# First attention and gate units of a two-block network: softmax, turned copies and a polynomial rearranged

## The reference

```python
# sliding-window attention, 32 query heads of 64, 4 key/value heads, blocks of 128 tokens
logits = jnp.where(valid, q @ k * (HEAD_DIM ** -0.5) + bias, NEG_INF)
m = jnp.maximum(jnp.max(logits, axis=-1, keepdims=True), sink)
e = jnp.exp(logits - m)
p = e / (jnp.sum(e, axis=-1, keepdims=True) + jnp.exp(sink - m))
o = p @ v
# the recurrent unit's gate
y_a = (rec * jax.nn.gelu(lru_gate, approximate=True)) @ w_lru_out
```

## Time and profile before

| | us |
|---|---|
| median of 3 runs | 2642.24 |
| lowest, highest | 2641.92, 2642.67 |
| the profiled execution | 2639.21 |
| its span in the profile | 2637.3 |
| granted TensorE clock, mean | 0.999 |

### The profile page before, as it was taken

The page is one execution under the profiler, slowest core; times in us unless marked ns, Lnnn a source line. Parts: engine busy times, 40 slices in busy tenths (PEclk is TensorE's granted clock), DMA queues, the critical chain, the costliest instruction groups (busy, mean ns, idle before and its releaser), DMA issues.

```text
span 2637.3 us, 35369 instructions
## 1 busy us (share of the span) xinstructions
PE 2612.8 (99%) x13718; PEld 2230.5 (85%) x13718; DVE 1840.2 (70%) x2519; ACT 1373.8 (52%) x2012; POOL 78.1 (3%) x136
## 2 busy tenths in 40 slices
PE   9999989999999999999999999999999999999998
PEld 7888878888888888888888888888888888888886
DVE  7876788888888786655665566676566566865665
ACT  5137766655444654454445445644655565445543
POOL 0000000000000000000000000100010001000000
PEclk9999999999999999999999999999999999999999
DMA  9995577788989696655565565565546646655463
GB/s 390 409 359 177 157 250 253 264 306 296 324 320 341 209 318 208 199 189 187 192 196 189 190 203 170 181 214 188 167 146 196 226 159 195 220 189 163 144 223 128
DMA packets 164727, 595.85 MB, mean 226 GB/s; under 512 B 19392, under 2 KB 20448, under 8 KB 164048
## 3 DMA queue, kind: packets, MB, share of 16 engines
q1 hardware_dynamic: 158544, 574.00, 64.1%
q0 software_dynamic: 6016, 19.59, 2.5%
HBM read 584.80 MB, written 3.47 MB: 223 GB/s over the span
## 4 chain that ended last, share of the span: by engine, by line
PE 90%; DVE 5%; ACT 3%; issue 1%; DMA 1%; SPq 0%; DVEq 0%; ACTq 0%
PE bank L839 27%; PE bank L881 26%; PE bank L893 14%; PE bank L844 13%; PE bank L856 2%; DVE both_w L1708 1%; PE pX L856 1%; PE pS L856 1%; PE pX L988 1%; PE pS L927 1%; ACT both_w L1255 1%; DMA raw<-in_w_vw 1%; PE pX L976 0%; PE pS L949 0%; DVE bank L2234 0%
## 5 line engine op out<-in xcount | busy, mean ns | idle before, releaser
L1708 DVE TENSOR_TENSOR both_w<-raw,both_w 128x1024 fp32r<-128x1024 f32 x848 | 1024.0, 1217 | 517.6 <-ACT both_w L1255 513.2
L1255 ACT ACTIVATE both_w<-raw 128x1024 fp32r<-128x1024 f32 x848 | 882.0, 1050 | 654.0 <-PE bank L844 407.1
L881 PE MATMUL bank<-H,both_w 128*128 128x512 f32 x3264 | 784.3, 391 | 0.1
L881 PEld LDWEIGHTS bank<-H,both_w 128*128 128x128 f32 x3264 | 599.3, 188 | 117.2 <-issue 1.3
L893 PE MATMUL bank<-H,both_w 128*128 128x256 f32 x3264 | 442.9, 285 | 0.7 <-DVE both_w L1708 0.7
L893 PEld LDWEIGHTS bank<-H,both_w 128*128 128x128 f32 x3264 | 424.4, 191 | 21.1 <-issue 2.0
L839 PE MATMUL bank<-both_w,H 128*128 128x512 f32 x1280 | 320.7, 393 | 0.4 <-DVE H L1711 0.3
L839 PEld LDWEIGHTS bank<-both_w,H 128*128 128x128 f32 x1280 | 238.6, 188 | 53.1 <-ACT both_w L1255 3.3
L839 PE MATMUL bank<-both_w,F 128*128 128x512 f32 x1024 | 253.1, 389 | 0.0
L1760 DVE SCALAR_TENSOR_TENSOR raw<-raw,CR 128x1024 f32<-128x1024 f32 x192 | 232.0, 1218 | 12.3 <-DMA raw<-in_ada 11.8
L839 PEld LDWEIGHTS bank<-both_w,F 128*128 128x128 f32 x1024 | 192.2, 188 | 39.9
(11 more groups left out here) (336 smaller groups left out, 2251.1 us busy)
## 6 DMA issues: line engine op xcount, KB each, us to landing
raw<-in_w_in SPq DMA_DIRECT2D x280, 512.0 KB, 3.7
raw<-in_w_ff SPq DMA_DIRECT2D x256, 512.0 KB, 4.1
raw<-in_ada SPq DMA_DIRECT2D x192, 512.0 KB, 5.6
raw<-in_w_out SPq DMA_DIRECT2D x96, 512.0 KB, 4.9
raw<-in_w_vw SPq DMA_DIRECT2D x64, 512.0 KB, 4.1
raw<-in_w_sig SPq DMA_DIRECT2D x64, 512.0 KB, 4.7
raw<-in_w_x SPq DMA_DIRECT2D x32, 512.0 KB, 10.3
raw<-in_w_lru_out SPq DMA_DIRECT2D x32, 512.0 KB, 4.7
```

Source lines behind the costliest of these rows:

```text
L881: ins = pe.matmul(out[i].rearrange("p (a s) -> p a s", a=2), whi[:, s, at_:at_ + 128], both[:, :, kt, :], start=(c == 0 and k == 0), stop= ...
L1255: act.activation(whi[:, s, 0:el.n], raw[el.slot][:, 0:el.n], ACT.Copy).then_inc(s_hi, 1)
L1708: dve.tensor_tensor(wlo[:, s, 0:n], raw[el.slot][:, 0:n], v32(whi[:, s, 0:n]), ALU.subtract).then_inc(s_lo, 1)
```

## The change

In the program's VectorE part, `softmax` with a sink reduces to the negated maximum at once (as the call without a sink did), takes the minimum with the negated sinks, and subtracts: three small instructions behind the bias step where there were four. The sinks are negated once, in place, in the first norm's stage. The two `inverse` calls of a block become one `inverse_both`, on both halves' columns, in the later of the two ticks. In the gate unit, 0.5 G1 (x^2 + G0/G1) x is formed as one instruction (x^2 + G0/G1) x, and the factor 0.5 G1 becomes the scale of the tanh.

In ScalarE's part, the two copies into PT move ahead of the exponentials of half 1, from tick 5 to tick 4. The scaling of half 0 moves from tick 5 to tick 0 of the next block, where both halves are now scaled together.

```diff
@@ ScalarE, attention
                 if 0 <= advance - 1 < NB:
-                    weigh(2 * advance - 1, 2 * advance - 1, S)
+                    for t in range(2):
+                        weigh(2 * advance - 2 + t, 2 * advance - 2 + t, 128 * (t + 1))
                 yield
...
                 yield from ticks(2)
-                for t in range(2):
-                    if advance < NB:
-                        exps(2 * advance + t, 2 * advance + t, 128 * (t + 1), True)
-                    yield
+                if advance < NB:
+                    exps(2 * advance, 2 * advance, 128, True)
+                yield
                 if 0 <= advance - 1 < NB:
...
                     act.activation(PT[:, 1, 0:2, :], pO[:, 256:512].rearrange("p (a q) -> p a q", q=128),
                                    ACT.Copy).then_inc(s_pt, 2)
                 if advance < NB:
-                    weigh(2 * advance, 2 * advance, 128)
+                    exps(2 * advance + 1, 2 * advance + 1, S, True)
+                yield
                 yield
@@ ScalarE, gate
-            act.activation(g1, g0, ACT.Tanh).then_inc(s_gt2, 1)
+            act.activation(g1, g0, ACT.Tanh, scale=0.5 * G1).then_inc(s_gt2, 1)
@@ VectorE, decay
+            sinks = vec[:, V_SINK:V_SINK + 32]
+            vc.add(dve.tensor_scalar(sinks, sinks, -1.0, None, ALU.mult))
@@ VectorE, softmax
-            t = vc.add(dve.tensor_reduce(mx, L, AX.X, ALU.max))
+            t = vc.add(dve.tensor_reduce(nm, L, AX.X, ALU.max, negate=True))
             dve.wait_ge(s_vc, t)
-            t = vc.add(dve.tensor_tensor(mx, mx, sink, ALU.max))
+            t = vc.add(dve.tensor_tensor(nm, nm, sink, ALU.min))
             dve.wait_ge(s_vc, t)
-            t = vc.add(dve.tensor_scalar(nm, mx, -1.0, None, ALU.mult))
+            dve.tensor_tensor(es, nm, sink, ALU.subtract).then_inc(s_mx, 1)
+
+        def inverse(a):
+            dve.wait_ge(s_ex, a + 1)
+            dve.reciprocal(SM[:, a % 4, 4, :], SM[:, a % 4, 2, :]).then_inc(s_rd, 1)
+
+        def inverse_both(b):
+
+            n = 2 * b % 4
+            rs, es, rd = (SM[:, n:n + 2, i, :] for i in (2, 3, 4))
+            dve.wait_ge(s_ex, 2 * b + 2)
+            t = vc.add(dve.tensor_tensor(rs, rs, es, ALU.add))
             dve.wait_ge(s_vc, t)
-            dve.tensor_tensor(es, sink, nm, ALU.add).then_inc(s_mx, 1)
-
-        def inverse(a, sink):
...
+            dve.reciprocal(rd, rs).then_inc(s_rd, 2)
@@ VectorE, attention
-                for t in range(2):
-                    inverse(2 * b + t, True)
-                    yield
+                yield
+                inverse_both(b)
+                yield
@@ VectorE, gate unit's evacuation
-                t = vc.add(dve.tensor_scalar(g0, g0, 0.5 * G1, 0.5 * G0, ALU.mult, ALU.add))
-                dve.wait_ge(s_vc, t)
-                dve.tensor_tensor(g0, g0, ps[:, :], ALU.mult).then_inc(s_gb, 1)
+                dve.scalar_tensor_tensor(out=g0, in0=g0, scalar=G0 / G1, in1=ps[:, :], op0=ALU.add, op1=ALU.mult).then_inc(s_gb, 1)
```

More of the change, by code:

```diff
@@ L1880, in softmax @@
             L, n = LP[:, jn % 3, :, 0:nk], a % 4
-            mx, nm, es = SM[:, n, 0, :], SM[:, n, 1, :], SM[:, n, 3, :]
+            nm, es = SM[:, n, 1, :], SM[:, n, 3, :]
             dve.wait_ge(s_qk, a + 1)
@@ L1897, in softmax @@
                 return
-            t = vc.add(dve.tensor_reduce(mx, L, AX.X, ALU.max))
+            t = vc.add(dve.tensor_reduce(nm, L, AX.X, ALU.max, negate=True))
             dve.wait_ge(s_vc, t)
-            t = vc.add(dve.tensor_tensor(mx, mx, sink, ALU.max))
+            t = vc.add(dve.tensor_tensor(nm, nm, sink, ALU.min))
             dve.wait_ge(s_vc, t)
-            t = vc.add(dve.tensor_scalar(nm, mx, -1.0, None, ALU.mult))
-            dve.wait_ge(s_vc, t)
-            dve.tensor_tensor(es, sink, nm, ALU.add).then_inc(s_mx, 1)
-        def inverse(a, sink):
-            rs, es, rd = SM[:, a % 4, 2, :], SM[:, a % 4, 3, :], SM[:, a % 4, 4, :]
-            dve.wait_ge(s_ex, a + 1)
-            if sink:
-                t = vc.add(dve.tensor_tensor(rs, rs, es, ALU.add))
-                dve.wait_ge(s_vc, t)
-            dve.reciprocal(rd, rs).then_inc(s_rd, 1)
+            dve.tensor_tensor(es, nm, sink, ALU.subtract).then_inc(s_mx, 1)
[7 more added lines that the diff above has]
+            t = vc.add(dve.tensor_tensor(rs, rs, es, ALU.add))
+            dve.wait_ge(s_vc, t)
+            dve.reciprocal(rd, rs).then_inc(s_rd, 2)
         def attention():
@@ L1971, in layer_jobs @@
                     elif job.a >= 0 and step == 1:
-                        inverse(job.a, False)
+                        inverse(job.a)
                 yield
```

## The result

| | median us | range | runs |
|---|---|---|---|
| before | 2642.45 | 2641.92 to 2644.05 | 4 |
| after | 2628.15 | 2627.65 to 2628.33 | 4 |

The ratio is 0.9945 with a 95% interval of 0.9927 to 0.9962: faster by 14.3 us. Forecast were 12.1 us, and 2630.1 us. The fast edge of the forecast's range, 2628.0, stood for a gain of 14.2 us, so the measured gain is just beyond it. The profiled execution of after took 2628.28 us, its span is 2626.4 us and its granted clock 0.999.

What follows compares the result with a forecast made beforehand. TensorE bounds the kernel, with 10.8 of its 24.5 idle us in the first attention. Waits 10.19, clock 1.67 and VectorE 0.25 sum to 12.11 us, so 2642.24 - 12.11 = 2630.1 us; range 2628.0 to 2635.5.

Steps and rivals of the forecast that it cites:

- All five waits: First attention, 310 to 550 us: TensorE's waits for L1358 ahead of L976 all go, 10.19 us.
- bounds of 1 to 2 us: VectorE's steps alone, without the moved copies, would bring about 1 to 2 us.
- no new wait: TensorE's transposes (L963): scaling both halves together adds no wait; bounds nothing or 0.5 us.
- the first place: Block 0, ahead of L976: copies into PT come in time, the 3.19 us wait goes, 0.6 us to spare.
- In the second: Transposes after the 3.94 us wait: the second scaling ends 0.5 to 1.3 us before TensorE comes.
- priced at 0.25 us: VectorE's shorter steps: the split that TensorE waited for at 328.25 us comes earlier, 0.25 us.
- the clock term: First attention, 391 to 396 us, behind the 3.94 us wait: the lowered clock goes with the wait, 1.67 us.
- clock luck: Rival: timed runs before met no fall (2631.8 us) or one at both long waits (2628.4); inside the forecast's 0.73.
- the offset of 3.03 us: Whole run: the median before lies 3.03 us above the profiled execution; the same difference was assumed after.
- not 13.7: VectorE's busy time over the run: 13.7 us less, 13.9 removed less 0.17 for negating the sinks.
- these prices: VectorE: the fused gate instruction takes L2246's time, no price; the merged reciprocal on 4 columns takes 0.17 us.
- nothing given back, and not slower: Rivals: DMA paces later weight stages, 2642 us (0.08 with no effect); joint reciprocal slips 5 us, 2656 us (0.05).

Runs made afterwards that it cites:

- e1_copies: Kernel before with only the two copies into PT moved ahead of the exponentials of half 1: 2630.05 us, ratio 0.9954.
- e11_order: Kernel before with all of ScalarE's new order, joint scalings included, VectorE's part old: 2630.15 us, ratio 0.9958.
- e9_filled: Kernel before with 7 and 8 products of unused result put into TensorE's two long waits: 2638.92 us, ratio 0.9989.
- e8_again: Kernel before, unchanged, for a second profiled execution: 2642.64 us.
- e10_again: Kernel before, unchanged, for a third profiled execution: 2640.31 us.
- e7_after: Kernel after, unchanged, run once more beside the kernel before: 2628.31 us, ratio 0.9948.
- e6_scaling: Kernel after with its scalings parted again, half 0 scaled at its old place in tick 5: 2631.31 us, ratio 0.9959.
- e2_vector: Kernel after with ScalarE's attention in the old order, so VectorE's steps alone: 2640.85 us, ratio 0.9997.
- e3_first: Kernel before with the copies into PT moved ahead in block 0 alone: 2637.26 us, ratio 0.9982.
- e4_second: Kernel before with the copies into PT moved ahead in block 2 alone: 2638.0 us, ratio 0.9983.
- e5_filled: Kernel before with 13 and 16 products of unused result put ahead of TensorE's two long waits: 2644.24 us, ratio 1.0008.

## Why the prediction was right and where it was wrong

**Right: the mechanism and its place.** All five waits of the earlier trace rows are gone, L1357 stands ahead of the second exponentials, and the stage is shorter by 12.1 us between the two profiled executions, as summed. e1_copies alone brings 12.0 us, and VectorE's steps alone 1.2 by the medians, in the bounds of 1 to 2 us that were set for them, though not told from nothing by the interval.

**Right, but by a smaller margin than it looks: no new wait.** In the first place 0.6 us to spare were worked out and 0.9 found. In the second, 0.5 to 1.3 us were worked out for the scalings and 1.7 found, but that was the wrong wait. What is last there is the copy into AT, with 0.0 us to spare; with the copies moved and VectorE's steps old it is late by 1.1 to 1.7 us (e1_copies, e11_order). The forecast was saved by a part of the change that it had priced at 0.25 us.

**Wrong: the clock term of the sum.** This is the step that failed. It was put at 1.67 us, one fall behind the second wait. The text said that this was shown once, and that the timed runs "may have paid for none, one or two"; then it took the one of the profiled execution. As a price of that one execution it was about right (1.5 us by its stage). For the timed runs e9_filled measured 3.1 us (0.3 to 5.3); the profiled executions show 3.7 us in e8_again and 1.6 in e10_again. With the 3.9 us by which e8_again stands above a sum without falls (1.67, and the 2.2 by which its stage is longer), the sum is 10.19 + 0.25 + 3.9 = 14.3 us, which is the timed difference; with the 3.1 us of e9_filled it is 13.5. The rival "clock luck" had the mechanism right, with 2628.4 us for falls at both waits. (Its sum, 2642.24 - 13.78, gives 2628.5, and the prediction names the edge of the range as 2627.9 in one place and 2628.0 in another; neither matters.) It was kept as the edge of the range, when a fall behind the first wait too was common.

**Wrong: the offset of 3.03 us, the same error from its other side.** The prediction added "the same difference" between the profiled execution and the median to the time after. The profiled execution of before was faster than all 64 timed ones. Against e8_again, 3.43 us above it, it began its stage 1.13 us sooner and had a stage shorter by 2.2; 0.1 is the rest. The sooner start was luck of that execution (the profiled ones begin the stage at 310.18 to 311.74 us, whatever the kernel), and to add it back was right: the kernel after began at 311.46. The 2.2 us are the clock term again. They belong to the waits and go with them, so they were not to be added back. The profiled execution of after, 2628.28 us, is 0.1 us off its median. That it began its stage at 311.46 us, and not at 310.83 as in e7_after, is chance too, so these shares of the 3.03 us are those of single executions.

**Wrong by 2 us, without weight:** VectorE is 11.7 us less busy, not 13.7. The merged instructions of after (count, ns min/median/max):

```profile
L1916 DVE TENSOR_TENSOR SM<-SM x16: 155/158/164, 331.2 to 611.8; 128x4 f32<-128x4 f32 x16
...
L1918 DVE RECIPROCAL SM<-SM x16: 178/179/180, 331.5 to 612.0; 128x4 f32<-128x4 f32 x16
...
L2250 DVE SCALAR_TENSOR_TENSOR TG<-TG,bank x8: 686/689/690, 323.7 to 487.4; 128x512 f32<-128x512 f32 x8
```

The fused gate step costs no more than the multiplication it replaces, and four columns cost 4 and 13 ns more than two: these prices were right. Added up instruction by instruction, VectorE's durations are 1938.9 us before and 1926.3 us after, 12.6 less. The busy time counts only once what two instructions overlap, so that small instructions can take less of it than their length: it falls by 11.7.

**Right: nothing given back, and not slower.** The rest behind the stage is 1994.4 us against 1994.5, and 1995.1 in e7_after. The sooner start of the weight stages cost nothing that stands out of this spread of about 1 us. The slip of the joint reciprocal did not reach TensorE in the kernel after; e6_scaling shows the part of it that could.

**Open.** Why a wait of 3.2 us is followed by a low clock in one execution and not in the next is not settled; the runs show only that it happens and what it costs. Differences of 1 to 2 us between variants are smaller than the intervals of their ratios (0.08 to 0.14% to either side, 2 to 4 us), the experiments ran on three different chips, and what is said of such differences stands on the traces and medians.

## What to carry to other kernels

Copies whose inputs are long ready belong into the hole that the same engine has anyway while it waits for another; look for it in the row ahead of the late instruction. Before the gain is summed, ask for each place where the waiting engine will arrive sooner not only whether the instruction that the change touches is in time, but which of all the instructions it waits for, those in the same memory bank too, comes last. And where a profiled execution lies outside the timed runs, do not carry the difference over: profile the kernel a second time and see which stage the difference is in.

## What the runs showed of the hardware

- Behind a wait of TensorE of 3.2 or 3.9 us the clock can fall to its lower level, 1.2 GHz (means of 0.57 to 0.74 over 5 us). Where it did, some 1.5 to 2.4 us were lost, 0.4 to 0.6 of the wait again. All the profiled executions with these waits left empty had it at least once; behind which wait changed from one to the next (e8_again, e10_again, e2_vector, e3_first, e4_second). Useless products in the waits brought 3.1 us (e9_filled).
- A float32 product of 128x128 by 128x256 takes 0.44 us and stands in the trace as two records: 26 records of 5.77 us for 13 products (e5_filled), where some 0.22 us had been reckoned.
- The profiled executions begin the stage 310.18 to 311.74 us after the span's start, those of the one kernel before 310.18 to 311.31 and of the kernel after 310.83 to 311.46. So 1.5 us of spread lie ahead of the stage; of the change only the one negation of the sinks stands there.
